# Where the sum of squares and the indexer's dots stand in TensorE's order, in a two-layer decoder trunk

## The chip, the cores and the metric

One NeuronCore of a Trainium2 chip runs the whole program in one launch. The metric is the device time of that launch in microseconds. TensorE multiplies matrices, VectorE and ScalarE move and transform results, GpSimd works on SBUF only, and SyncE issues the loads of the weights. The engines run side by side and wait for each other through semaphores.

## The reference

Two layers over 512 tokens of width 1024. Each layer has two gated feed-forward halves (width 2816) with a mixing stage between them.

```python
x = x + 0.5 * swiglu(rms_norm(x, ffn1_norm[l]), ffn1_gate[l], ffn1_up[l], ffn1_down[l])
h = rms_norm(x, mix_norm[l])
z = h @ w_in[l]         # queries, keys, values, indexer queries (4 heads), key, weights, pool, memory queries
# indexer, per block of 128 queries: dots = iq . ik ; score = sum_h w_h * relu(dots_h) ; top 128 keys
x = x + concat(y_attn, y_pool, y_mem) @ w_out[l]
x = x + 0.5 * swiglu(rms_norm(x, ffn2_norm[l]), ffn2_gate[l], ffn2_up[l], ffn2_down[l])
```

`rms_norm` divides by the root of the mean square over the 1024 channels. The kernel multiplies first and divides afterwards, when a product leaves PSUM, so the projections can start before the sum of squares is known.

## The kernel before, in words

Everything is float32. A matrix product takes three passes, high by high, high by low and low by high, where the high part is rounded to the multiplier's format by ScalarE and the low part is the rest (`passes`, L448; every matmul is recorded at L446). The activations are kept with channels on the partitions: 8 chunks of 128 channels by 512 tokens.

Weights come in slots of 128 x 1024 through a ring of four. SyncE loads a slot (L348), ScalarE rounds it (`round_ahead`, L883 to L891) when the slot's old user on TensorE is done (`slot_done`), GpSimd makes the low half (L382) and raises `w_ready`. One slot holds the weights of 24 matmuls. In ScalarE's program the roundings stand between the other work, so a rounding also waits for its turn.

A phase is a feed-forward half or a mixing stage; there are six. Each begins with `prepare`: ScalarE makes the high half of the activations and squares them (L871), VectorE makes the low half (L1097) and adds the squares of the 8 chunks in three additions (L1103 twice, L1105). TensorE starts with `project_first` (L462), which takes the first two slots and needs only the halves, and then `token_sums` (L508), one matmul with a matrix of ones into bank 4 that sums over the partitions. `root` (L877) takes the square root on ScalarE, `invert` (L1108) the reciprocal `r` on VectorE. Each evacuation multiplies by `r`.

In a feed-forward half the first gate and up products fill banks 0 and 1, the second (`gate_up(0, 1)`) banks 2 and 3. The first gate product in the loop may start when banks 0 and 1 are evacuated (`gu_free`, raised at L1138).

In the mixing stage the order on TensorE is: indexer queries (two slots, banks 0 and 1), the token sums, indexer key (bank 2), head weights (bank 3), value slots 0 and 1 (`project_v`, 8 blocks of three matmuls a slot, into banks 4 to 7), the transposition of `r` and of the head weights into columns (L612 to L618), the dots, value slots 2 and 3, the memory's sum, and then the query and key projections (`project_z`), into banks 0 to 3 in turn. Behind the third query slot, TensorE issues `heads_sum(0)` (L575), which needs the squares of the first query tile (ScalarE, L975), and that tile must first be evacuated by VectorE (L1156).

The dots are 12 products (three query blocks 1 to 3, four heads) of 256, 384 or 512 columns with a contraction over 64 rows. Heads 0 and 2 are on partitions 0 to 63, heads 1 and 3 on 64 to 127. They use banks 0 and 1 alternately, and product n waits for the ReLU of n - 2 (L952). ScalarE writes the ReLU to one of two buffers, VectorE adds it times its head weight to the score (L1193). VectorE then takes the largest scores, 8 at a time in 16 rounds (`take_largest`, L1199): six rounds ahead of the first query evacuation, then one round behind each.

All of it is in program order per engine; nothing is scheduled at run time.

Of the kernel before, what the change touches and what calls it, by code (L numbers as in the profile page):

```python
# [106 lines left out]
def build(nc, x_t, mem_t, weights, pool_w, params, consts, spreads, out):  # L107
# [93 lines left out]
    def sem(name):  # L201
        return nc.alloc_semaphore(name)
# [41 lines left out]
    mv_ready = sem("mv_ready")  # L244
    idx_hi_ready = sem("idx_hi_ready")
    idx_lo_ready = sem("idx_lo_ready")
    dots_done = sem("dots_done")
    relu_ready = sem("relu_ready")
    acc_score = sem("acc_score")
    bias_ready = sem("bias_ready")  # L250
# [89 lines left out]
    with nc.Block() as block:  # L340
# [103 lines left out]
        def _(pe):  # L444
# [10 lines left out]
            def weight(pos, at, n=P):  # L455
                s = slice(pos * SLOT + at, pos * SLOT + at + n)
                return w_hi[:, s], w_lo[:, s]
# [4 lines left out]
            def project_first(l, ph, n):  # L462


                def with_hi(i, k, part):
                    mm(bank[i][:, :], weight((n + i) % RING, k * P)[part], chunk(h_hi, k),
                       part == 0 and k == 0, False)

                def rounded(k):
                    pe.wait_ge(hi_ready, (l * 3 + ph) * DC + (k + 1))  # L470

                if ph == 0:

                    pe.wait_ge(w_hi_done, l * SLOTS + (n + 1))
                    for k in range(DC):
                        rounded(k)
                        with_hi(0, k, 0)
                        if k == 0:
                            pe.wait_ge(w_ready, l * SLOTS + (n + 1))
                        with_hi(0, k, 1)  # L480
                    pe.wait_ge(w_ready, l * SLOTS + (n + 2))
                    for k in range(DC):
                        for part in range(2):
                            with_hi(1, k, part)
                else:
                    pe.wait_ge(w_ready, l * SLOTS + (n + 2))
                    for k in range(DC):
                        rounded(max(k, 1))
                        for i in range(2):
                            for part in range(2):  # L490
                                with_hi(i, k, part)
                for i in range(2):
                    for k in range(DC):
                        if i == 0:
                            pe.wait_ge(lo_ready, (l * 3 + ph) * DC + (k + 1))
                        last = mm(bank[i][:, :], weight((n + i) % RING, k * P)[0], chunk(h_lo, k),
                                  False, k == DC - 1)
                    last.then_inc(slot_done, 1)
# [9 lines left out]
            def token_sums(l, ph):  # L508

                pe.wait_ge(consts_loaded, 16)  # L510
                pe.wait_ge(ssq_ready, l * 3 + (ph + 1))
                mm(bank[4][:, :], con(C_ONES, P), chunk(sq, 0)).then_inc(sum_done, 1)
# [11 lines left out]
            def ffn(l, e):  # L524
                ph, ffn_at = 2 * e, FFN_BASE[e]

                def gate_up(f, half):
                    n = ffn_at + 2 * half

                    pe.wait_ge(gu_free, (l * 2 + e) * FC + (f + (half + 1)))  # L530
                    at = l * SLOTS + ffn_at + f * 2 + 2 * half
                    for up in range(2):
                        pos = (n + up) % RING
                        pe.wait_ge(w_ready, at + (up + 1))
                        for k in range(DC):
                            last = passes(bank[2 * half + up][:, :], weight(pos, k * P),
                                          pair(h_hi, h_lo, k * T), k == 0, k == DC - 1)
                        last.then_inc(slot_done, 1)


                pe.wait_ge(gu_free, (l * 2 + e) * FC + 1)
                project_first(l, ph, ffn_at)
                token_sums(l, ph)
                gate_up(0, 1)
                with pe.Fori(1, FC // 2) as i:
                    gate_up(i * 2, 0)
                    gate_up(i * 2, 1)


                down_at = ffn_at + 2 * FC  # L550
                def down(f, off, start=False, stop=False, **part):
                    at = l * SLOTS + down_at + f + off
                    pe.wait_ge(w_ready, at + 1)

                    pe.wait_ge(a_lo_ready, (l * 2 + e) * FC + (f + (off + 1)))
                    fo = f * T + off * T
                    pos = (down_at + off + (f if isinstance(f, int) else 0)) % RING
                    accumulate(pos, a_hi[:, ds(fo, T)], a_lo[:, ds(fo, T)], start, stop, **part)

                pe.wait_ge(rms_ready, l * 3 + (ph + 1))  # L560
                down(0, 0, start=True, banks=range(4, DC))
                pe.wait_ge(gu_free, (l * 2 + e) * FC + (FC + 2))
                down(0, 0, start=True, banks=range(4), at=4)
                down(0, 1)
                with pe.Fori(0, (FC - 2) // RING - 1) as i:
                    for off in range(RING):
                        down(i * RING, 2 + off)
                for off in range(RING):
                    down(FC - RING, off, stop=off == RING - 1)

            def mix(l):
                def at(name, i=0):
                    return MIX_BASE[name] + i
# [14 lines left out]


                project_first(l, 1, at("iq"))  # L590
                token_sums(l, 1)
                project(l, at("ik"), bank[2][:, :], h_hi, h_lo)
                project(l, at("iw"), bank[3][:, :], h_hi, h_lo)

                pe.wait_ge(rms_ready, l * 3 + 2)

                def project_v(s):
                    n = at("av", s)
                    pe.wait_ge(w_ready, l * SLOTS + (n + 1))
                    for half in range(2):  # L600
                        k = 2 * s + half
                        whi, wlo = weight(n % RING, half * T, T)
                        for i in range(TT):
                            hhi, hlo = pair(h_hi, h_lo, k * T + i * P, P)
                            last = passes(bank[4 + i][:, :], (hhi, hlo), (whi, wlo),
                                          k == 0, k == DC - 1)
                    last.then_inc(slot_done, 1)

                project_v(0)
                project_v(1)  # L610
# [6 lines left out]
                              con(C_ID, 4, 4))  # L617
                last.then_inc(cols_done, 1)  # L618

                n = 0  # L620
                pe.wait_ge(idx_lo_ready, (l + 1) * 3)
                for i in range(1, TT):
                    for h in range(IDX_HEADS):
                        if n >= 2:
                            pe.wait_ge(relu_ready, l * 12 + (n - 1))
                        p0 = HD * (h % 2)
                        at_q = (h // 2) * T + i * P
                        q = [t[p0:p0 + HD, at_q:at_q + P] for t in (idx_hi, idx_lo)]
                        k = [t[p0:p0 + HD, 2 * T:2 * T + (i + 1) * P] for t in (idx_hi, idx_lo)]
                        passes(bank[n % 2][:, 0:(i + 1) * P], q, k, True, True)\  # L630
                            .then_inc(dots_done, 1)
                        n += 1
                project_v(2)
                project_v(3)

                pe.wait_ge(mssq_ready, l + 1)
                mm(bank[2][:, 0:MEM], con(C_ONES, P), sq[:, 0:MEM]).then_inc(msum_done, 1)


                def project_z(t, name, i):  # L640

                    if t < 6:
                        pe.wait_ge(relu_ready, (l + 1) * 12)
                    elif t == 6:
                        pe.wait_ge(mrms_ready, l + 1)
                    elif t == 7:
                        pe.wait_ge(cols_ready, l + 1)
                    else:
                        pe.wait_ge(proj_ready, l * 17 + (t - 3))
                    project(l, at(name, i), bank[t % 4][:, :], h_hi, h_lo)  # L650

# [206 lines left out]
        def _(act):  # L858
# [61 lines left out]
            def mix(l):  # L920
# [25 lines left out]
                n = 0  # L946
                for i in range(1, TT):
                    for h in range(IDX_HEADS):
                        act.wait_ge(dots_done, l * 12 + (n + 1))
                        if n >= 2:  # L950
                            act.wait_ge(acc_score, l * 12 + (n - 1))
                        nc.scalar.activation(chunk(t2, n % 2, T, (i + 1) * P), bank[n % 2][:, 0:(i + 1) * P],  # L952
                                             ACT.Relu, scale=HD ** -0.5 * IDX_HEADS ** -0.5)\
                            .then_inc(relu_ready, 1)
                        n += 1
# [501 lines left out]
```

## Time and profile before

| what | us |
| --- | --- |
| median of 3 runs | 2082.27 |
| lowest and highest of them | 2079.69 and 2084.04 |
| span of the profiled execution, first to last instruction | 2078.0 |
| TensorE busy in it | 2041.0 |
| VectorE, ScalarE, GpSimd busy | 755.7, 793.8, 891.0 |

The profile gives one execution. Of that execution only the span is listed, no separate time; the runs' median lies 4.3 above the span. Times in rows are microseconds from the start of the span. A matmul's end is modelled, so consecutive matmuls overlap in the rows.

### The profile page before, as it was taken

What the parts mean: (1) busy time and instruction counts of PE and PEld (TensorE: products, weight loads), DVE (VectorE), ACT (ScalarE), POOL (GpSimd) and SP (SyncE); (2) the same over time, 40 slices, a digit from 0 to 9 for tenths busy, and PEclk for the clock granted to TensorE, in tenths of its full rate; (3) what the DMA queues carried; (4) which work ended last, traced back from release to release, by engine and by line L of the source; (5) the groups of instructions that cost most, each with busy time, mean ns of one, the idle gap of its engine ahead of it and who ended that gap; (6) DMA issues with size and microseconds to landing.
All of it is one profiled execution on the core that took longest, in us unless ns stands there. A gap on an engine that the chain in (4) does not pass through costs nothing.

```text
span 2078.0 us, 27450 instructions
## 1 busy us (share of the span) xinstructions
PE 2041.0 (98%) x9256; PEld 1632.0 (79%) x9256; DVE 755.7 (36%) x1180; ACT 793.8 (38%) x1064; POOL 891.0 (43%) x404
## 2 busy tenths in 40 slices
PE   6999999999999999999989999999999999999999
PEld 5888888776767788888878888887767677888887
DVE  5333300675441633330063333006854425333201
ACT  5434321532452544432154443215325535444311
POOL 4444444433612444444354444444337034444442
PEclk9999999989899999999999999999899999999999
DMA  4222222312011222222222222223120022222222
GB/s 173 101 91 97 95 102 95 115 69 74 21 42 52 91 100 92 101 91 101 91 82 101 91 101 91 101 94 115 62 81 21 32 71 91 93 99 91 101 101 101
DMA packets 50567, 182.55 MB, mean 88 GB/s; under 512 B 5752, under 2 KB 6008, under 8 KB 50240
## 3 DMA queue, kind: packets, MB, share of 16 engines
q1 hardware_dynamic: 49824, 178.84, 24.7%
q10 hardware_dynamic: 672, 2.80, 0.4%
q8 instruction: 40, 0.66, 0.1%
q14 instruction: 31, 0.25, 0.0%
HBM read 179.52 MB, written 2.10 MB: 87 GB/s over the span
## 4 chain that ended last, share of the span: by engine, by line
PE 95%; DVE 3%; ACT 1%; issue 0%; DMA 0%; DVEq 0%; SPq 0%; ACTq 0%
PE bank L446 93%; PE bank L784 2%; DVE sq L1103 2%; DVE h_lo L1097 1%; DVE sq L1105 1%; ACT h_hi L863 0%; DMA x<-x_t 0%; ACT sq L871 0%; DVE x L1120 0%; DVEq L1097 0%; ACT t L952 0%; ACT L863 0%; DVEq L1096 0%; SPq L353 0%; ACTq L863 0%
## 5 line engine op out<-in xcount | busy, mean ns | idle before, releaser
L382 POOL TENSOR_TENSOR w_lo<-raw,w_hi 128x1024 fp32r<-128x1024 f32 x328 | 824.4, 2515 | 1141.8 <-ACT w_hi L891 1141.2
L891 ACT ACTIVATE w_hi<-raw 128x1024 fp32r<-128x1024 f32 x329 | 348.4, 1060 | 868.5 <-PE bank L446 868.0
L446 PE MATMUL bank<-h_hi,w_hi 128*128 128x512 f32 x1664 | 657.6, 395 | 12.0 <-ACT h_hi L863 12.0
L446 PE MATMUL bank<-h_hi,w_lo 128*128 128x512 f32 x1664 | 650.1, 391 | 0.0
L446 PE MATMUL bank<-h_lo,w_hi 128*128 128x512 f32 x1664 | 634.5, 390 | 0.0
L446 PEld LDWEIGHTS bank<-h_hi,w_hi 128*128 128x128 f32 x1664 | 314.3, 189 | 94.0 <-issue 16.2
L446 PEld LDWEIGHTS bank<-h_lo,w_hi 128*128 128x128 f32 x1664 | 313.9, 189 | 66.8 <-issue 2.4
L446 PEld LDWEIGHTS bank<-h_hi,w_lo 128*128 128x128 f32 x1664 | 314.1, 189 | 65.8
L446 PE MATMUL bank<-a_hi,w_hi 128*128 (+2 forms) x864 | 334.3, 387 | 0.0
L446 PE MATMUL bank<-a_hi,w_lo 128*128 (+2 forms) x864 | 332.8, 385 | 0.0
L446 PE MATMUL bank<-a_lo,w_hi 128*128 (+2 forms) x864 | 332.8, 385 | 0.0
L1120 DVE SCALAR_TENSOR_TENSOR x<-bank,x 128x512 f32<-128x512 f32 x48 | 32.7, 692 | 503.8 <-PE bank L446 503.8
L1138 DVE TENSOR_TENSOR t<-bank,r 128x512 f32<-128x512 f32 x88 | 60.8, 691 | 384.0 <-PE bank L446 384.0
L1144 DVE TENSOR_TENSOR a_lo<-t,a_hi 128x512 f32 x88 | 167.6, 1905 | 81.0 <-ACT a_hi L908 81.0
L446 PEld LDWEIGHTS bank<-a_hi,w_hi 128*128 128x128 f32 x864 | 162.3, 188 | 34.0 <-issue 2.1
L446 PEld LDWEIGHTS bank<-a_hi,w_lo 128*128 128x128 f32 x864 | 162.3, 188 | 32.6
L446 PEld LDWEIGHTS bank<-a_lo,w_hi 128*128 128x128 f32 x864 | 162.4, 188 | 32.0
L891 ACT ACT_TABLE_LOAD x45 | 57.7, 1283 | 138.7 <-PE bank L446 131.2
L1135 DVE TENSOR_TENSOR t<-bank,r 128x512 f32<-128x512 f32 x88 | 60.8, 691 | 91.5 <-PE bank L446 89.8
L908 ACT ACTIVATE a_hi<-t 128x512 f32 x88 | 55.6, 632 | 48.5 <-DVE t L1142 48.5
L1142 DVE TENSOR_TENSOR t<-t,t 128x512 f32<-128x512 f32 x88 | 61.3, 697 | 10.8
L905 ACT ACTIVATE t<-t 128x512 f32<-128x512 f32 x88 | 54.9, 624 | 12.6 <-DVE t L1135 12.1
(137 smaller groups left out, 1446.3 us busy)
## 6 DMA issues: line engine op xcount, KB each, us to landing
raw<-weights SPq DMA_DIRECT2D x332, 512.0 KB, 3.2
x<-x_t SPq DMA_DIRECT2D x4, 512.0 KB, 6.9
mem<-mem_t ACTq DMA_DIRECT2D x2, 1024.0 KB, 4.9
out_t<-x SPq DMA_DIRECT2D x8, 256.0 KB, 2.6
const<-consts SPq DMA_DIRECT2D x1, 505.5 KB, 9.8
spread_in<-spreads ACTq DMA_DIRECT2D x2, 216.0 KB
wpool<-pool_w ACTq DMA_DIRECT2D x2, 128.0 KB, 4.7
par<-params SPq DMA_DIRECT2D x1, 38.0 KB, 1.9
```

Of the source, the lines that this page charges most:

```text
L382: G.tensor_tensor(out=w_lo[:, s], in0=raw[:, s], in1=w_hi[:, s].bitcast(f32), op=ALU.subtract).then_inc(w_ready, 1)
L446: return nc.tensor.matmul(out_, lhsT, rhs, start=start, stop=stop, skip_group_check=True)
L784: last = nc.tensor.transpose(bank[2 + n % 2][:, b * P:(b + 1) * P], prob[n % 4][:, b * P:(b + 1) * P], con(C_ID, P))
L891: nc.scalar.activation(w_hi[:, s], raw[:, s], ACT.Copy).then_inc(w_hi_done, 1)
L905: nc.scalar.activation(g, g, ACT.Silu).then_inc(silu_ready, 1)
L908: nc.scalar.activation(a_hi[:, ds(f * T + half * T, T)], chunk(t2, half), ACT.Copy).then_inc(a_hi_ready, 1)
L1103: link(l, V.tensor_tensor(out=sq[:, 0:half], in0=sq[:, 0:half], in1=sq[:, half:2 * half], op=ALU.add))
L1120: V.scalar_tensor_tensor(out=chunk(x, j), in0=bank[j][:, :], scalar=scale, in1=chunk(x, j), op0=ALU.mult, op1=ALU.add)\
L1135: V.tensor_tensor(out=g, in0=bank[2 * half][:, :], in1=r[:, :], op=ALU.mult).then_inc(gate_ready, 1)
L1138: V.tensor_tensor(out=h, in0=bank[2 * half + 1][:, :], in1=r[:, :], op=ALU.mult).then_inc(gu_free, 1)
L1142: V.tensor_tensor(out=h, in0=g, in1=h, op=ALU.mult).then_inc(prod_ready, 1)
L1144: V.tensor_tensor(out=a_lo[:, ds(f * T + half * T, T)], in0=h, in1=a_hi[:, ds(f * T + half * T, T)].bitcast(f32), op=ALU.subtract).then_in ...
```

## The change

In a feed-forward half, `token_sums` is issued inside `gate_up(0, 1)`, after its gate matmuls and ahead of its up matmuls. In the mixing stage it is issued behind the projection of the indexer key.

The dots are split by query block. `dots(1)` stands ahead of value slot 2, `dots(2)` ahead of the block (1, 1) of slot 2, and `dots(3)` ahead of the block (0, 2) of slot 3. Each group writes banks 0 to 3, one for each head, and issues pass by pass, with the two heads of a pair alternating. Groups 2 and 3 wait once, for the four ReLUs of the group before. The wait for the columns' copy and the wait for all twelve ReLUs move ahead. There are two semaphores for finished dots, for even and for odd heads. Which operations run, and on what sizes, stays the same.

```diff
-                def gate_up(f, half):
+                def gate_up(f, half, between=None):
...
                         last.then_inc(slot_done, 1)
+                        if between is not None and up == 0:
+                            between()
...
                 project_first(l, ph, ffn_at)
-                token_sums(l, ph)
-                gate_up(0, 1)
+                gate_up(0, 1, lambda: token_sums(l, ph))
...
                 project_first(l, 1, at("iq"))
+                project(l, at("ik"), bank[2][:, :], h_hi, h_lo)
                 token_sums(l, 1)
-                project(l, at("ik"), bank[2][:, :], h_hi, h_lo)
                 project(l, at("iw"), bank[3][:, :], h_hi, h_lo)
...
+                        for i in range(TT):
+                            if before is not None and (half, i) in before:
+                                dots(before[half, i])
+                            last = v_block(n, s, half, i)
...
+                def dots(i):
+
+                    if i >= 2:
+                        pe.wait_ge(relu_ready, l * 12 + (i - 1) * IDX_HEADS)
+                    for hp in range(0, IDX_HEADS, 2):
+                        at_q = (hp // 2) * T + i * P
+                        for part, (tq, tk) in enumerate(((idx_hi, idx_hi), (idx_hi, idx_lo),
+                                                         (idx_lo, idx_hi))):
+                            for half in range(2):
+                                p = slice(half * HD, (half + 1) * HD)
+                                last = mm(bank[hp + half][:, 0:(i + 1) * P], tq[p, at_q:at_q + P],
+                                          tk[p, 2 * T:2 * T + (i + 1) * P], part == 0, part == 2)
+                                if part == 2:
+                                    last.then_inc(dots_done[half], 1)
...
-                n = 0
                 pe.wait_ge(idx_lo_ready, (l + 1) * 3)
-                for i in range(1, TT):
-                    for h in range(IDX_HEADS):
-                        if n >= 2:
-                            pe.wait_ge(relu_ready, l * 12 + (n - 1))
...
-                        passes(bank[n % 2][:, 0:(i + 1) * P], q, k, True, True)\
-                            .then_inc(dots_done, 1)
-                        n += 1
-                project_v(2)
-                project_v(3)
+                pe.wait_ge(cols_ready, l + 1)
+                project_v(2, {(0, 0): 1, (1, 1): 2})
+                project_v(3, {(0, 2): 3})
 
                 pe.wait_ge(mssq_ready, l + 1)
+                pe.wait_ge(relu_ready, (l + 1) * 12)
...
-                        act.wait_ge(dots_done, l * 12 + (n + 1))
+                        act.wait_ge(dots_done[h % 2], l * 6 + (n // 2 + 1))
...
-                        nc.scalar.activation(chunk(t2, n % 2, T, (i + 1) * P), bank[n % 2][:, 0:(i + 1) * P],
+                        nc.scalar.activation(chunk(t2, n % 2, T, (i + 1) * P), bank[h][:, 0:(i + 1) * P],
```

## Rows read from the trace of the kernel before

**Rows 1.** The page's busy line: us, share of the span, instructions.
```profile
PE 2041.0 (98%) x9256; PEld 1632.0 (79%) x9256; DVE 755.7 (36%) x1180; ACT 793.8 (38%) x1064; POOL 891.0 (43%) x404
```
**Rows 2.** Waits of TensorE: line waited for, us in total, times, longest.
```profile
PE bank L446 <- DVE sq L1105: 19.5, 6, 5.5
```
**Rows 3.** Timeline, TensorE, phase starts: start, us, instruction, [idle before, releaser].
```profile
29.12 1.97 PE L446 MATMUL bank<-sq,const 128*128 128x512 f32 x2 [3.99 <-DVE sq L1105]
...
394.46 2.08 PE L446 MATMUL bank<-sq,const 128*128 128x512 f32 x2 [3.50 <-DVE sq L1105]
...
690.29 3.79 PE L446 MATMUL bank<-h_lo,w_hi 128*128 128x512 f32 x16
695.55 1.12 PE L446 MATMUL bank<-sq,const 128*128 128x512 f32 x2 [1.47 <-DVE sq L1105]
...
1061.79 2.08 PE L446 MATMUL bank<-sq,const 128*128 128x512 f32 x2 [5.53 <-DVE sq L1105]
...
1427.91 1.30 PE L446 MATMUL bank<-sq,const 128*128 128x512 f32 x2 [3.50 <-DVE sq L1105]
```
**Rows 4.** Timeline, VectorE: evacuation of the second up product in three gate/up phases.
```profile
42.84 0.69 DVE L1138 TENSOR_TENSOR t<-bank,r 128x512 f32<-128x512 f32 x1 [1.24 <-PE bank L446]
...
707.62 0.69 DVE L1138 TENSOR_TENSOR t<-bank,r 128x512 f32<-128x512 f32 x1 [0.46 <-PE bank L446]
...
1076.29 0.69 DVE L1138 TENSOR_TENSOR t<-bank,r 128x512 f32<-128x512 f32 x1 [1.92 <-PE bank L446]
```
**Rows 5.** Timeline, ScalarE, VectorE, GpSimd behind the sum of the phase at 695.
```profile
696.71 0.69 ACT L880 ACTIVATE r<-bank,const 128x512 f32<-128x512 f32 x1 [6.07 <-PE bank L446]
...
697.43 3.35 DVE L1110 RECIPROCAL r<-r 128x512 f32<-128x512 f32 x1 [1.94 <-ACT r L880]
...
701.82 0.68 DVE L1138 TENSOR_TENSOR t<-bank,r 128x512 f32<-128x512 f32 x1
...
699.85 2.40 POOL L382 TENSOR_TENSOR w_lo<-raw,w_hi 128x1024 fp32r<-128x1024 f32 x1 [6.16 <-ACT w_hi L891]
```
**Rows 6.** Timeline, GpSimd: low half of ring slot 2, first phases of both layers.
```profile
21.69 3.55 POOL L382 TENSOR_TENSOR w_lo<-raw,w_hi 128x1024 fp32r<-128x1024 f32 x1 [4.60 <-ACT w_hi L891]
...
1052.84 5.07 POOL L382 TENSOR_TENSOR w_lo<-raw,w_hi 128x1024 fp32r<-128x1024 f32 x1 [4.60 <-ACT w_hi L891]
```
**Rows 7.** Timeline, mixing stage of layer one up to the column matmuls.
```profile
397.16 3.29 ACT L933 ACTIVATE a_hi<-mem,par 128x256 fp32r<-128x256 f32 x8
...
403.80 1.90 ACT L937 ACTIVATE sq<-mem 128x2048 f32<-128x2048 f32 x1
...
415.72 0.67 DVE L1156 TENSOR_TENSOR iw<-bank,r 4x512 f32<-4x512 f32 x1
...
418.96 1.05 PE L446 MATMUL bank<-const,r 1*128 1x1 f32 x8
```
**Rows 8.** Timeline, TensorE: first dots, first dot of block 3, return to the values.
```profile
420.83 0.39 PE L446 MATMUL bank<-idx_hi 64*128 64x256 f32 x2
...
427.22 0.79 PE L446 MATMUL bank<-idx_hi 64*128 64x512 f32 x1
...
431.79 0.80 PE L446 MATMUL bank<-w_hi,h_hi 128*128 128x512 f32 x1
```
**Rows 9.** Timeline: last score, first round, query evacuation, its square, its head sum.
```profile
432.83 0.75 DVE L1193 SCALAR_TENSOR_TENSOR score<-t,cols,score 128x512 f32<-128x512 f32 x1 [0.22 <-DVE score L1193]
434.09 1.48 DVE L1206 MAX8 top<-score 128x8 f32<-128x512 f32 x3 [0.51 <-DVE score L1193]
...
453.54 0.62 DVE L1156 TENSOR_TENSOR z<-bank,r 128x512 f32<-128x512 f32 x1
...
454.19 0.63 ACT L975 ACTIVATE t<-z 128x512 f32<-128x512 f32 x1 [2.51 <-DVE z L1156]
...
461.38 1.04 PE L446 MATMUL bank<-t,const 128*20 128x512 f32 x2
```
**Rows 10.** Busy us by engine in one stretch, then granted clock, DMA share, GB/s.
```profile
421.70:435.40 13.70, 13.26 (x39) 9.59 (x40) 9.18 (x15) 6.93 (x13) 0.86 (x1) 0.50 0.11 39
```

More of the change, by code:

```diff
@@ L246, in build @@
     idx_lo_ready = sem("idx_lo_ready")
-    dots_done = sem("dots_done")
+    dots_done = [sem("dots_even_done"), sem("dots_odd_done")]
     relu_ready = sem("relu_ready")
@@ L590, in mix, with v_block, project_v @@
                 project_first(l, 1, at("iq"))
+                project(l, at("ik"), bank[2][:, :], h_hi, h_lo)
                 token_sums(l, 1)
-                project(l, at("ik"), bank[2][:, :], h_hi, h_lo)
                 project(l, at("iw"), bank[3][:, :], h_hi, h_lo)
                 pe.wait_ge(rms_ready, l * 3 + 2)
-                def project_v(s):
+                def v_block(n, s, half, i):
+                    k = 2 * s + half
+                    hhi, hlo = pair(h_hi, h_lo, k * T + i * P, P)
+                    return passes(bank[4 + i][:, :], (hhi, hlo), weight(n % RING, half * T, T),
+                                  k == 0, k == DC - 1)
+                def project_v(s, before=None):
                     n = at("av", s)
@@ L600, in project_v @@
                     for half in range(2):
-                        k = 2 * s + half
-                        whi, wlo = weight(n % RING, half * T, T)
                         for i in range(TT):
-                            hhi, hlo = pair(h_hi, h_lo, k * T + i * P, P)
-                            last = passes(bank[4 + i][:, :], (hhi, hlo), (whi, wlo),
-                                          k == 0, k == DC - 1)
+                            if before is not None and (half, i) in before:
+                                dots(before[half, i])
+                            last = v_block(n, s, half, i)
                     last.then_inc(slot_done, 1)
+                def dots(i):
[11 more added lines that the diff above has]
+                                    last.then_inc(dots_done[half], 1)
                 project_v(0)
@@ L618, in mix @@
                 last.then_inc(cols_done, 1)
-                n = 0
                 pe.wait_ge(idx_lo_ready, (l + 1) * 3)
-                for i in range(1, TT):
-                    for h in range(IDX_HEADS):
-                        if n >= 2:
-                            pe.wait_ge(relu_ready, l * 12 + (n - 1))
[L626 to L629, printed above, removed]
-                        passes(bank[n % 2][:, 0:(i + 1) * P], q, k, True, True)\
-                            .then_inc(dots_done, 1)
-                        n += 1
-                project_v(2)
-                project_v(3)
+                pe.wait_ge(cols_ready, l + 1)
+                project_v(2, {(0, 0): 1, (1, 1): 2})
+                project_v(3, {(0, 2): 3})
                 pe.wait_ge(mssq_ready, l + 1)
+                pe.wait_ge(relu_ready, (l + 1) * 12)
                 mm(bank[2][:, 0:MEM], con(C_ONES, P), sq[:, 0:MEM]).then_inc(msum_done, 1)
                 def project_z(t, name, i):
-                    if t < 6:
-                        pe.wait_ge(relu_ready, (l + 1) * 12)
-                    elif t == 6:
+                    if t == 6:
                         pe.wait_ge(mrms_ready, l + 1)
-                    elif t == 7:
-                        pe.wait_ge(cols_ready, l + 1)
-                    else:
+                    elif t >= 8:
                         pe.wait_ge(proj_ready, l * 17 + (t - 3))
```

## The prediction

> **What bounds the kernel now.** I read the page's busy line first: TensorE is busy 98% of a span of 2078.0 us, no other engine over 43% [rows 1]. So the time is TensorE's instruction count times its pace, plus what stops it. The list of who waited for whom leaves one stop that matters: TensorE waits for the last addition of the sum of squares, six times, 19.5 us in all [rows 2]. The timeline of TensorE at five of the six phase starts shows each: 3.99, 3.50, 1.47, 5.53 and 3.50 us idle before the matmul with the ones (the sixth repeats the third) [rows 3]. A matmul's row is 0.39 us long but the next starts after (3.79-0.39)/15 = 0.227 us [rows 3], so an "idle" of the profile understates the lost time by 0.16. I call T0 the moment at which the array could take the next matmul: sum row, minus idle, minus 0.16, which gives 24.97, 390.80, 693.92 and 1056.10.
>
> 24 matmuls (one weight slot) take 5.44 us at that pace. In the second gate/up phase the evacuation of the second pair starts at 707.62 [rows 4]: 13.70 after T0 = 1.63 wait + 10.88 for two slots + 1.19. Of the 1.19 I give 1.0 to the sum itself and 0.2 to the release of the reader. The same subtraction for the first phase gives 17.87 = 4.15 + 10.88 + 1.19 + 1.65 left, and for layer two 20.19 = 5.69 + 10.88 + 1.19 + 2.43 left [rows 3, 4]. What is left is half clock after the wait.
>
> The second place is the indexer's dots: 36 small matmuls hold TensorE from 420.83 to 431.79 [rows 8], and the granted clock there and in the value projection behind it is 0.50 for 13.7 us [rows 10], its lower level of 1.2 GHz. Between dots TensorE waits for ScalarE to empty one of two banks.
>
> **Edit one, gate/up phases.** The gate's 24 matmuls go ahead of the wait. Before, both halves (10.88 us) covered the chain from the sum to the freed bank; now only the up half does. That chain, from [rows 3, 5]: sum at 695.55, square root on ScalarE at 696.71, reciprocal on VectorE 697.43 to 700.78, gate and up evacuated by 701.82 + 0.68 = 702.50: 6.95 us, with its release 7.0. Cover is 1.0 + 5.44 = 6.44, so a new wait of about 0.55 us arises at the first looped gate. Its weights are no later: the low half on GpSimd ends at 699.85 + 2.40, 6.70 after the sum. So the next gate starts at (end of moved gate) + 7.0, against (evacuation row - 0.2) before.
> - First phase: slot 2 of the ring is ready at 21.69 + 3.55 = 25.24 [rows 6], 0.3 after T0. 25.28 + 5.44 + 7.0 = 37.72 against 42.64: 4.9 saved.
> - Second gate/up phase of a layer: slot ready. 693.92 + 5.44 + 7.0 = 706.36 against 707.42: 1.1 saved, twice.
> - Layer two's first: the slot is ready only at 1052.84 + 5.07 = 1057.91 [rows 6], so 1.8 of the wait stays as a wait for weights. 1057.95 + 12.44 = 1070.39 against 1076.09: 5.7 saved.
>
> Sum: 12.7 us. No DMA changes order; weight loads are released by rounding, which follows TensorE, and land in a few us against 5.44 per slot.
>
> **Edit two, key projection ahead of the sum.** T0 = 390.80. Keys to 396.24 (the sum's input was ready at 394.4, no wait left), sum to 397.2, head weights to 402.7, two value slots to 413.5. Before, they ended just ahead of 418.96 [rows 7]: 5.4 earlier. But the column matmuls wait for the evacuation of the head weights, which ended at 415.72 + 0.67 = 416.39, at the end of VectorE's queue: additions over the memory's squares, eight low halves, three index low halves. Its start hangs on ScalarE's square of the memory at 403.80 [rows 7], which waited for the key slot; now it follows square root (397.4), eight high halves (3.29) and one rounding (1.06), so about 402.2, 1.6 earlier. The evacuation ends at about 414.8: a new wait of 1.3 us. Columns 1.9 us [rows 7, 8], then about 0.3 for the copy that dots now wait for: the dots start at D = 417.1 against 420.83.
>
> **Edit three, dots.** Two heads sit in different halves of the rows. The first two products start together: two in 0.39 us [rows 8]. So 12 matmuls of 256, 384, 512 columns cost 6 pairs: 0.68, 1.02, 1.36 us at full clock, 3.06 together; one after the other they would be 6.12. Into and out of small products I add 0.35 a group (after the last one the next large matmul starts some 0.1 late, and the second product of a head some 0.1 late, by the spacing around [rows 8]). I take 4.1, near the pairs, since the row is of the same operation. Value slots 2 and 3 are 16 blocks of 0.68 = 10.88. They end at E = D + 15.0 = 432.1, against 431.79 + 10.88 + about 1.8 of half clock = 444.5: 12.4 earlier.
> Dots group 2 needs group 1's four activations. All twelve took 12.75 us before (420.83 to 432.83 + 0.75) [rows 8, 9], about 1.06 a head, 4.2 for four; it comes at D + 4.4. No wait.
>
> The Trainium skill ("TensorEngine Tiling (Array Packing)", Key Properties) says that changing the tiling mode drains TensorE, which speaks against splitting one stretch of small matmuls into three. The trace shows such a change as about 0.1 us. By the rule alone there are four more changes a layer, and at that price the sum loses under 1 us, which the 0.35 holds.
>
> **What is late next.** The selection on VectorE starts when the last score is added. Before, that was 433.58, 10.9 us ahead of the end of the value projection; now group 3 starts at D + 1.0 + 3.4 + 1.4 + 3.4 = D + 9.2. From its first matmul to the last addition were 6.4 us (427.22 to 433.58) at half clock, about 5.3 at full. Scores end at D + 14.5, only 0.5 ahead of E. Then 0.5, six rounds and a reciprocal up to the first query evacuation, 434.09 to 453.54 = 19.45, and its square ready 454.19 + 0.63 = 454.82, 1.3 behind [rows 9]: D + 35.75 = 452.85. TensorE reaches the first head sum, behind three query slots, at E + 0.3 + 16.4 = D + 31.7. New wait: about 4 us, where there were 6.5 us of slack. Head sum: 461.38 [rows 9] to 452.85, 8.5 saved. VectorE needs 3.6 a tile against 5.44 of TensorE, so it catches up and nothing waits again. Two layers: 17.0.
>
> Clock. A wait of 4.15 us cost 1.65 behind it, 5.69 cost 2.43, 1.63 cost nothing [rows 3, 4]. The new 4 us cost 1.65 a layer: 3.3. The 1.3 wait, the one-row column matmuls and the 0.3 are low activity like the stretch after which the clock fell at 421.7 [rows 10]; dots between full-size blocks should lift it. Bounds 0 and 2.4 a layer; I take 0.8: 1.6.
> The Trainium skill ("TensorE: Matmul & The Clock Gate", HAM oscillation) has it that idle gaps close the gate and the work behind them runs at half rate; the trace agrees for gaps of 3.66 us and up. By it the new wait costs what is charged above; without it the sum would be 3.3 better.
>
> **Sum.** 12.7 + 17.0 - 3.3 - 1.6 = 24.8 us off a span of 2078.0: 2053.2. Of the profiled execution only the span is given; the median of the runs, 2082.27, lies 4.3 above it. Forecast: 2057.5.
>
> **Rivals.**
> - A, the selection does not hold TensorE (it hides as it did). For it: VectorE had 6.5 us of slack. Against: that slack was made by the scores ending 10.9 us early. The gain is then that at E: 2 x 12.4 + 12.7 - 1.6 = 35.9: 2046.5.
> - B, the clock stays at half level through both value slots, since small matmuls now come three times. For it: four stretches of low activity in a row, [rows 10]. Against: 5 full blocks between groups, and the clock rose 3.6 us after blocks resumed at 431.79. 15.0 us of work become 28, E = D + 28, head sum at D + 45; 7.5 a layer worse than forecast, of which 1.6 is charged: 24.8 - 15 + 1.6 = 11.5: 2071. The Trainium skill (same page, psum-queue depth-cycling) has a kernel whose short idles between bank groups made the clock oscillate; that would be B.
> - C, slower: the same half clock reaches from the columns through the query slots to the first head sum. 31.7 us at 1.88 times is D + 59.6, against 461.38 = D + 44.3: 15.3 lost a layer; 30.6 - 12.7 = 18 slower: 2100. It decides from some 22 us of full-clock work per layer run at half. Before, the clock recovered each time within four us of dense work.
> - D, the change does not do what it says: the moved gate only moves the wait (the chain longer than 7.0, or weights late), leaving the mix gain alone or half of all: 12 us, 2070.
>
> **Chances.** Forecast 0.64 (its own range 2051 to 2064), A 0.12, B 0.12, C 0.05, D 0.07. Range 2046 to 2070: low end A, high end just short of B and D; their halves outside and C are about 0.15. A measurement tells no change within 0.2%, 4.2 us. Slower takes C: 0.05; within 0.2%, the tails of B and D: 0.04; faster 0.91.
>
> **What would show it.** Right: no wait for the sum of squares but 1.8 at layer two's weights; waits of 0.5 for the up evacuation, 1.3 for the head-weight evacuation, about 4 for the first query square; dots 4 us a layer; clock 1.00 in the value slots. Wrong: no wait at the first head sum (A), clock 0.5 over the value slots (B), a wait over 1.5 behind the up half (D).

## The result and the profile after

The changed kernel takes 2065.68 us (median of 4 runs, 2063.15 to 2067.45) against 2080.98 for the kernel before (4 runs). The ratio is 0.9924, 95% interval 0.9909 to 0.9938: 15.3 us faster. The profiled execution took 2067.45 with a span of 2065.6, so what lies around a span is 1.85 us. Its span is 12.4 under that of before.

The list of who waited for whom, for TensorE, the whole span (line waited for, us in total, times, longest); of before it showed [rows 2]:

```profile
PE bank L446 <- ACT h_hi L871: 12.0, 1, 12.0
PE bank L446 <- ACT t L983: 7.8, 2, 3.9
PE bank L446 <- DVE iw L1164: 6.5, 2, 3.2
PE bank L446 <- DVE t L1146: 2.1, 4, 0.6
PE bank L446 <- DVE h_lo L1105: 1.7, 1, 1.7
PE bank L446 <- DVE cols L1190: 0.9, 2, 0.5
```

The 19.5 us for the sum of squares are gone. Five kinds of wait have come: 3.9 a layer for the square of the first query tile, 3.2 a layer for the evacuated head weights, 0.5 four times for the up evacuation, 1.7 once for the low half of the activations, 0.45 a layer for the columns' copy. (The first line is the start of the program, 12.0 before too.)

TensorE in the timeline, first phase and the mixing stage of layer one (start, us, instruction, idle before); they answer to [rows 3, 7, 8, 9]:

```profile
21.98 3.79 PE L446 MATMUL bank<-h_lo,w_hi 128*128 128x512 f32 x16
...
31.05 1.02 PE L446 MATMUL bank<-sq,const 128*128 128x512 f32 x2
...
38.10 0.49 PE L446 MATMUL bank<-h_hi,w_hi 128*128 128x512 f32 x1 [0.55 <-DVE t L1146]
...
382.78 3.79 PE L446 MATMUL bank<-h_lo,w_hi 128*128 128x512 f32 x16
...
391.85 1.02 PE L446 MATMUL bank<-sq,const 128*128 128x512 f32 x2
...
412.47 1.05 PE L446 MATMUL bank<-const,r 1*128 1x1 f32 x8 [3.24 <-DVE iw L1164]
...
415.62 0.58 PE L446 MATMUL bank<-idx_hi 64*128 64x256 f32 x2 [0.45 <-DVE cols L1190]
...
427.18 0.50 PE L446 MATMUL bank<-idx_hi 64*128 64x512 f32 x2
...
428.44 0.40 PE L446 MATMUL bank<-idx_hi,idx_lo 64*128 64x512 f32 x2
428.76 0.50 PE L446 MATMUL bank<-w_hi,h_hi 128*128 128x512 f32 x1
```

With T0 as in the prediction (here 25.61, 386.41, 689.16, then 1052.5, 1413.23, 1711.69), the span's stages compare so:

| stage | before | after | saved | forecast |
| --- | --- | --- | --- | --- |
| start to first T0 | 24.97 | 25.61 | -0.6 | 0 |
| first gate/up half | 365.83 | 360.80 | 5.0 | 4.9 |
| mixing, layer one | 303.12 | 302.75 | 0.4 | 6.0 |
| second half and layer two's first | 730.33 | 724.07 | 6.3 | 6.8 |
| mixing, layer two | 298.86 | 298.46 | 0.4 | 6.0 |
| last half | 354.89 | 353.94 | 0.9 | 1.1 |

The gate/up phases gave 12.2 of the 12.7 forecast. The two mixing stages gave 0.8 of 12.1.

Inside layer one's mixing stage, counted from T0: the columns start at 26.06 (28.16 before, 24.04 forecast), the dots at 29.21 (30.03 before, 26.3 forecast), the first head sum at 67.43 (70.58 before, 62.05 forecast), and the next phase's T0 is at 302.75 (303.12). So of the forecast head start of 5.4 us, 3.3 are lost ahead of the columns and 1.3 more ahead of the dots, and of 3.15 saved at the head sum 2.8 are lost behind it.

**Ahead of the columns.** VectorE's and GpSimd's timeline, the first two of the eight low halves of the memory, each by itself, then the next two, and then GpSimd:

```profile
402.42 2.62 DVE L1178 SCALAR_TENSOR_TENSOR a_lo<-mem,par,a_hi 128x256 fp32r<-128x256 f32 x1
404.96 2.68 DVE L1178 SCALAR_TENSOR_TENSOR a_lo<-mem,par,a_hi 128x256 fp32r<-128x256 f32 x1
407.57 0.87 DVE L1178 SCALAR_TENSOR_TENSOR a_lo<-mem,par,a_hi 128x256 fp32r<-128x256 f32 x2
...
402.13 2.63 POOL L382 TENSOR_TENSOR w_lo<-raw,w_hi 128x1024 fp32r<-128x1024 f32 x1 [1.89 <-ACT w_hi L899]
404.97 2.39 POOL L382 TENSOR_TENSOR w_lo<-raw,w_hi 128x1024 fp32r<-128x1024 f32 x1 [0.22 <-ACT w_hi L899]
```

Each takes under 0.5 us where nothing is beside it (two in 0.87), and 2.6 where a GpSimd instruction runs: both end within 0.3 us of GpSimd's. The eight together took 7.60 us, against 5.42 before, when one GpSimd instruction fell on them. These 2.2 us are why the head weights came 1.9 to 2.1 us later than forecast. The Trainium skill ("GPSIMD Engine Reference", its table of specifications) names it: GpSimd shares its SBUF interfaces with VectorE, with contention for VectorE instructions that have two SBUF inputs. The trace agrees, and gives the price.

**From the columns to the scores, and behind the head sum.** Busy us by engine, then granted clock, DMA share, GB/s, four stretches of the changed kernel's layer one:

```profile
413.30:420.10 6.80, 6.35 (x29) 5.46 (x30) 2.12 (x5) 1.43 (x4) 0.72 (x1) 0.51 0.23 77
453.80:457.30 3.50, 3.46 (x7) 1.91 (x8) 3.50 (x11) 1.52 (x3) 2.38 (x1) 0.59 0.00 0
...
540.00:560.00 20.00, 20.00 (x118) 14.46 (x117) 7.08 (x21) 9.81 (x26) 17.49 (x24) 0.84 0.00 1
...
620.00:640.00 20.00, 20.00 (x92) 13.62 (x92) 4.54 (x16) 4.89 (x14) 0.00 (x0) 0.70 0.00 0
```

and two stretches of before that answer to the last two:

```profile
547.50:567.50 20.00, 20.00 (x86) 13.89 (x85) 5.85 (x17) 6.43 (x16) 16.66 (x23) 0.64 0.01 1
...
627.50:645.00 17.50, 17.50 (x106) 12.21 (x106) 5.57 (x22) 6.38 (x21) 0.00 (x0) 1.00 0.01 1
```

The clock was at its lower level from the column matmuls through the first dots into the value blocks, for 6.8 us where before it was for 13.7 [rows 10]; it fell again behind the wait at the head sum; and in the attention units, which the change doesn't touch, it was lower in one place and higher in another than before. The two stretches of before start 7.5 us later, as the head sum does.

**The selection.** The last score and the first query's evacuation (VectorE), its square (ScalarE) and its head sum (TensorE), as in [rows 9]:

```profile
431.80 0.75 DVE L1201 SCALAR_TENSOR_TENSOR score<-t,cols,score 128x512 f32<-128x512 f32 x1 [0.22 <-DVE score L1201]
433.06 1.48 DVE L1214 MAX8 top<-score 128x8 f32<-128x512 f32 x3 [0.51 <-DVE score L1201]
...
452.49 0.63 DVE L1164 TENSOR_TENSOR z<-bank,r 128x512 f32<-128x512 f32 x1
...
453.16 0.63 ACT L983 ACTIVATE t<-z 128x512 f32<-128x512 f32 x1 [13.01 <-DVE z L1164]
```

From last score to square ready are 21.24 us, exactly as before. The scores end 16.9 us after the first dots (12.75 before, 14.5 forecast).

### The profile page after: what moved, and what is told of

It reads as the page before. It is cut to its first block, busy times and chain, and to the rows that moved or that the text cites. A ratio compares the mean times of both kernels' runs of the same rounds, so it can differ in the third digit from the quotient of the medians.

```text
span 2065.6 us, 27440 instructions
## 1 busy us (share of the span) xinstructions
PE 2030.5 (98%) x9256; PEld 1625.5 (79%) x9256; DVE 762.3 (37%) x1180; ACT 791.8 (38%) x1064; POOL 889.0 (43%) x404
## 4 chain that ended last, share of the span: by engine, by line
PE 93%; DVE 3%; issue 2%; ACT 1%; DVEq 0%; DMA 0%; SPq 0%; ACTq 0%
PE bank L446 91%; PE bank L792 2%; DVE r L1118 1%; DVE a_lo L1178 0%; DMA x<-x_t 0%; DVE score L1201 0%; ACT a_hi L941 0%; DVE h_lo L1105 0%; DVE score L1217 0%; DVE top L1214 0%; DVE sq L1171 0%; ACT sq L945 0%; DVE idx_lo L1185 0%; ACT r L888 0%; ACT h_hi L871 0%
## 5 line engine op out<-in xcount | busy, mean ns | idle before, releaser
L446 PEld LDWEIGHTS bank<-h_hi,w_hi 128*128 128x128 f32 x1664 | 314.1, 189 | 96.9 <-issue 15.3
L913 ACT ACTIVATE t<-t 128x512 f32<-128x512 f32 x88 | 54.9, 624 | 12.6 <-DVE t L1143 12.1
```

What stands on the lines that cost most here:

```text
L446: return nc.tensor.matmul(out_, lhsT, rhs, start=start, stop=stop, skip_group_check=True)
L913: nc.scalar.activation(g, g, ACT.Silu).then_inc(silu_ready, 1)
```

## The experiments

Each ran in five rounds against the kernel before; the times of before in the three groups are 2082.34, 2079.94 and 2082.91. The differences from the changed kernel below are between medians of different groups, so 1 or 2 us in them mean nothing. "Up to the first head sum" is counted from the mixing stage's T0 in the profiled execution (70.6 and 70.9 us in the two layers of before, 67.4 in both of the changed kernel), "behind it" from there to the next phase's T0.

### Which edit brings what

Sum moved in the gate/up phases alone (the diff's edit to `gate_up` on the kernel before):

> The kernel before with the sum moved in the four gate/up phases alone. Theory (the gate/up edit brings nearly all, the mixing edits nearly nothing): span 12 us under the kernel before, about 2066, the same as the changed kernel within 2; four new waits of 0.55 us for the up evacuation; both mixing stages 303 and 299 us from first free slot to the next phase's, as before. Rival (the mixing edits bring their forecast share and the gate/up edit less): 5 us or less under the kernel before.

Measured: 2071.48, ratio 0.9952 (0.9935 to 0.9968). The profiled execution, the quickest of six, had a span of 2065.6, 12.4 under the profiled one of before. There are four waits for the up evacuation, 2.1 us together, and the mixing stages' two waits of 3.5 for the sum of squares stay. The gate/up stages up to layer two's mixing give 11.3 us, as in the changed kernel, which is what the theory says of them. Two things differ from it: the median is 5.8 us over the changed kernel's, not within 2, and the mixing stages took 298.8 and 301.4 us, not 303 and 299, though nothing was changed in them.

Both moves of the sum, dots as before:

```diff
                 project_first(l, 1, at("iq"))
+                project(l, at("ik"), bank[2][:, :], h_hi, h_lo)
                 token_sums(l, 1)
-                project(l, at("ik"), bank[2][:, :], h_hi, h_lo)
```

> Both moves of the sum, with the dots as they were: one stretch, two banks. Theory (the split of the dots takes from the mixing stage what the earlier key projection gives it): the wait for the head weights is there (3 us), the columns start some 2 us earlier than before, no wait at the first head sum, so 2 us a layer over the first experiment: 16 us under the kernel before, 2062, faster than the changed kernel by 3 to 4. Rival (split dots are a gain by themselves and the losses are elsewhere): 2068 to 2072, slower than the changed kernel.

Measured: 2067.46, ratio 0.9936 (0.9917 to 0.9956). Within its interval this is the changed kernel's time without the split dots. The wait for the head weights is there, 3.2 a layer, and there is none at the first head sum. It is not the 3 to 4 us faster than the changed kernel that I expected; the intervals can't tell which of the two is ahead. In the profiled executions the changed kernel is 2.4 us ahead in each layer up to the first head sum (67.4 against 69.8), and behind it this one is 7.6 us quicker over both layers, with the same instructions.

Split dots alone:

```diff
-                gate_up(0, 1, lambda: token_sums(l, ph))
+                token_sums(l, ph)
+                gate_up(0, 1)
...
+                token_sums(l, 1)
                 project(l, at("ik"), bank[2][:, :], h_hi, h_lo)
-                token_sums(l, 1)
```

> The split dots alone, both sums where they were. Theory (TensorE saves the dots' waits but gives them back at the first head sum, behind the selection, and in half clock): wait of 2 to 4 us at the first head sum, 0 to 2 us a layer saved, span 2074 to 2078. Rival (the split saves its 8 us a layer and only the head weights' wait eats it in the changed kernel): 2062 to 2064.

Measured: 2079.87, ratio 0.9987 (0.9978 to 0.9997): 2.7 us. It has the same 3.9 us wait at the first head sum in both layers, with no late head weights in the way. Up to the first head sum it saves 2.4 and 3.0 us. So the split by itself saves about 1 us a layer, and the late head weights can't be the reason, since there are none here.

### The wait for the head weights

In the changed kernel, ScalarE's roundings of value slot 3 and query slot 0 are held, so GpSimd's low halves come later:

```diff
+                act.wait_ge(proj_ready, l * 17 + 4)
                 round_ahead(l, MIX_BASE["iw"])
                 round_ahead(l, MIX_BASE["av"])
```

> The changed kernel with two of ScalarE's roundings (value slot 3, query slot 0) held until the head weights are evacuated, so that GpSimd's two low halves no longer run beside VectorE's eight low halves of the memory. Theory (a VectorE instruction that meets a GpSimd one waits for its end, two such meetings of 2.2 us): the eight take 3.4 us in place of 7.6, the wait for the head weights goes from 3.2 to under 0.5, the columns run at full clock, 3.5 to 6 us a layer faster than the changed kernel: 2054 to 2059. Rival (the eight are long for another reason, their input or ScalarE beside them): still 7 us, the wait stays near 3, no gain.

Measured: 2058.41, ratio 0.9883 (0.9864 to 0.9903), 7.3 us under the changed kernel. VectorE and GpSimd in its timeline:

```profile
402.83 3.26 DVE L1179 SCALAR_TENSOR_TENSOR a_lo<-mem,par,a_hi 128x256 fp32r<-128x256 f32 x8
...
413.04 1.70 DVE L1202 SCALAR_TENSOR_TENSOR score<-t,cols,const 128x256 f32<-128x256 f32 x1 [1.30 <-ACT t L961]
414.95 2.30 DVE L1202 SCALAR_TENSOR_TENSOR score<-t,cols,score 128x256 f32<-128x256 f32 x1 [0.22 <-DVE score L1202]
...
409.78 7.19 POOL L382 TENSOR_TENSOR w_lo<-raw,w_hi 128x1024 fp32r<-128x1024 f32 x3 [9.13 <-ACT w_hi L899]
```

All eight low halves take 3.26 us with GpSimd away, and no wait for the head weights is left. The collisions have moved to two score additions, 1.70 and 2.30 in place of 0.48, where the next group of dots is not yet due (one wait of 1.2 us in two layers). The edit moves ScalarE's roundings too, but in the changed kernel ScalarE stood idle from 404.89 to 409.27, while the second long low half ran (404.96 to 407.64). This settles the meeting with GpSimd as the cause of the late head weights.

### The wait at the first head sum

Selection rounds spread, in the changed kernel:

```diff
-FIRST_ROUNDS = ROUNDS - ZT
+FIRST_ROUNDS = 2
+TILE_ROUNDS = [2] * 4 + [1] * 6
...
-                    take_largest(l * DVE_CHAIN + links[0])
-                    links[0] += ROUND_CHAIN
+                    for _ in range(TILE_ROUNDS[j]):
+                        take_largest(l * DVE_CHAIN + links[0])
+                        links[0] += ROUND_CHAIN
```

> The changed kernel with VectorE's selection rounds spread: two ahead of the first query evacuation in place of six, two behind each of the first four tiles. Theory (the wait at the first head sum is the selection's six rounds, now 12 us shorter to the first tile): the wait of 3.9 us goes in both layers, and the half clock behind it; 4 to 6 us a layer, 2054 to 2058. No new wait, since two rounds and an evacuation (6.6) stand against a projection and a head sum (6.4), with 7 us of slack at the start. Rival (TensorE is held by something behind it, and the wait moves to the next head sums or to a bank): under 3 us in all.

Measured: 2059.22, ratio 0.9887 (0.9866 to 0.9907): 6.5 under the changed kernel. The wait is gone in both layers and none has come in its place. The gain is below the 8 to 12 us expected. Up to the first head sum the profiled execution saves 2.8 and 4.0 us; it had three long stretches of half clock in the attention units.

Groups of dots nearer:

```diff
-                project_v(2, {(0, 0): 1, (1, 1): 2})
-                project_v(3, {(0, 2): 3})
+                project_v(2, {(0, 0): 1, (0, 3): 2})
+                project_v(3, {(0, 0): 3})
```

> The changed kernel with three blocks between the first two groups of dots and five before the third, in place of five and five. Theory (the scores end later because VectorE idles 4.3 us between groups 1 and 2 and 1.7 between 2 and 3): scores end about 1.5 to 2.5 us earlier after the first dots, the wait at the first head sum falls to 1.5 to 2.5 us, 1.4 to 2.5 us a layer, 2061 to 2064. Rival (TensorE then waits for the activations ahead of group 2): a new wait of 1 us or more there and no gain.

Measured: 2064.74, ratio 0.9917 (0.9899 to 0.9935), not to be told from the changed kernel. The wait fell from 7.8 to 5.1 us for both layers, 2.6 a layer where 1.5 to 2.5 was expected:

```profile
PE bank L446 <- ACT t L983: 5.1, 2, 2.6
```

The spacing sets when the scores end, but 1.3 us a layer is too little to show.

### Both remedies

The held roundings and the spread rounds together:

> The held roundings and the spread selection together. Theory (two separate waits, one behind the other on TensorE): the gains add, 7 from the held roundings and 8 to 12 from the selection, 2046 to 2051; no wait over 1.3 us in the mixing stages but the columns' copy. Rival (the first saving is taken back at the second place): not below 2055.

Measured: 2045.14 (2043.23 to 2047.89), ratio 0.9828 (0.9809 to 0.9847). This is the best version, 20.5 us under the changed kernel, more than the 7.3 and 6.5 of the two remedies alone. TensorE's waits in it:

```profile
PE bank L448 <- ACT h_hi L873: 12.1, 1, 12.1
PE bank L448 <- DVE t L1149: 2.1, 4, 0.5
PE bank L448 <- POOL w_lo L384: 1.9, 2, 1.7
PE bank L448 <- DVE cols L1193: 0.9, 2, 0.5
```

Its mean granted clock is 0.992, of the changed kernel 0.988: 17 us less at the lower level (2 x 0.008 x 2043 = 33 against 2 x 0.012 x 2066 = 50), worth about half of that, 8 us, by estimate. The surplus of 6.7 us is of that size. Up to the first head sum the two gains nearly add: 9.5 and 6.8 us over both layers apart, 17.2 together. The rest of the surplus arises behind it, where the two layers took 461.8 us, against 466.2 to 467.4 in the changed kernel and with either remedy alone. That this comes of the remedies and not by chance is not shown.

Not all of the half clock ahead of the value slots goes with the late head weights. The best version in layer one, behind its first dots (busy us by engine, clock, DMA share, GB/s):

```profile
411.80:415.10 3.30, 3.30 (x18) 2.59 (x15) 2.26 (x2) 1.04 (x3) 3.30 (x2) 0.52 0.49 159
```

That is 3.3 us at the lower level in place of 6.8; the columns ran at 1.00. (In layer two of the run with the held roundings alone the clock stayed at 1.00 there, so the fall is not certain either.)

With the groups nearer as well:

> The last one with the groups nearer as well. Theory (with the selection no longer holding TensorE, where the groups stand does not matter): the same as without, within 2 us. Rival (nearer groups make TensorE wait for the activations): 2 to 4 us slower.

Measured: 2054.67 (2049.94 to 2058.69), ratio 0.9875 (0.9853 to 0.9897): 9.5 slower than without, so the theory fell. TensorE now waits for the activations ahead of a group:

```profile
PE bank L448 <- ACT t L963: 3.8, 2, 2.5
```

That is 3.8 us; GpSimd's held instructions stand on the score additions that those activations follow. The mean clock is 0.988, which by the same estimate is 8 us, so the two more than cover the loss.

Old dots, both moves of the sum, held roundings, the selection as before:

> Both moves of the sum and the held roundings, with the dots in one stretch on two banks as before and the selection as before. Theory (once its two waits are taken away, the split of the dots is worth what was forecast for TensorE, some 5 to 8 us a layer): this stands at the second experiment's time less 5 to 7, about 2061, that is 12 to 17 us slower than the split dots with both remedies (2045). Rival (the split is worth little even then, and the held roundings and the rest do it): within 6 us of 2045.

Measured: 2066.74, ratio 0.9927 (0.9907 to 0.9947): 21.6 slower than the best version, where I expected 12 to 17. The held roundings gave next to nothing here, 0.7 us. Their collisions fall on score additions which the old dots wait for one by one:

```profile
PE bank L446 <- ACT t L954: 6.7, 6, 1.5
```

Up to the first head sum the best version is 10.0 us a layer ahead of this one (58.8 against 68.8), and that is nearly all of the difference. There was no wait at the head sum here for spread rounds to take away. So with its two waits removed the split of the dots is worth about 10 us a layer. Against the kernel before, the best version reaches the head sum 11.8 and 12.1 us earlier: that is close to rival A, which had 12.4 less 0.8 for the clock.

Heads of a pair one after the other in the best version:

```diff
-                        for part, (tq, tk) in enumerate(...):
-                            for half in range(2):
+                        for half in range(2):
+                            for part, (tq, tk) in enumerate(...):
```

> The version with both remedies, but within a group each head's three products are issued in a row, as before, in place of the two heads of a pair alternating. Theory (heads of a pair overlap only when their instructions alternate, since now no wait separates the pairs): a group of 512 columns takes 2.2 to 2.7 us in place of 1.6, 2 to 3 us a layer on TensorE, 2049 to 2051. Rival (the two halves of the rows overlap in either order, as the kernel before showed for its first two heads): no difference, 2045 within 2.

Measured: 2047.49, ratio 0.9828 (0.9813 to 0.9843), the same. The two row halves overlap in either order; in the kernel before only the wait between the two heads had kept them apart. Its third group of dots:

```profile
423.16 0.50 PE L448 MATMUL bank<-idx_hi 64*128 64x512 f32 x2
423.49 0.40 PE L448 MATMUL bank<-idx_lo,idx_hi 64*128 64x512 f32 x2
423.73 0.40 PE L448 MATMUL bank<-idx_hi,idx_lo 64*128 64x512 f32 x2
```

## Why the prediction was right or wrong

The direction was right and 2065.68 lies in the range of 2046 to 2070, but outside the 2051 to 2064 of the forecast itself, nearer to rival D's 2070, whose mechanism did not happen. The forecast of 2057.5 gave 24.8 us where 15.3 came. From span to span, which is what the sum was made of, only 12.4 came, half of it. The two profiled executions lie differently in their runs (2079.85 and 2067.45 beside medians of 2080.98 and 2065.68), and adding 4.3 us to a span, where 1.85 lies around it, made the forecast 2.4 too long. So the number missed by 8.2 and the sum by 12.4. By its steps:

1. **The wait for the sum of squares goes, a chain of 7.0 us takes its place: right.** Sum at 31.05, next gate at 38.10: 7.05. New wait 0.55, four times. 12.2 us for 12.7.
2. **Layer two's slot of weights keeps 1.8 of the wait: right in size, but in the profiled execution by luck.** There the low half of the activations met GpSimd and cost a wait of 1.70, the weights none. The first experiment shows the forecast form, 1.7 for `w_lo`.
3. **"The evacuation ends at about 414.8: a new wait of 1.3 us": this term was mis-sized.** The wait was 3.2 (3.4 from slot to slot). The sum took the eight low halves at their 5.42 us of before. Of that duration 2.2 were a collision (3.26 without any), and moving TensorE ahead moved GpSimd's next instruction onto them too. The held roundings show it. 2.1 us a layer.
4. **The dots cost 4.1 us of TensorE: right.** Group 3 took 428.76 - 427.18 = 1.58 for 1.7, group 2 the same way 1.3 for 1.4.
5. **"Bounds 0 and 2.4 a layer; I take 0.8" for half clock: mis-sized.** Columns and first dots ran at half clock for 6.8 us, columns to dots took 3.15 us for the 2.2 taken, and the scores came 2.4 us later behind the first dots than forecast. That is 3.3 us in layer one and 3.2 in layer two, above the upper bound. The late head weights are about half of it: without them 3.3 us at the lower level are left in the best version, which cost 1.6, still twice the 0.8.
6. **A wait of about 4 us at the first head sum: right,** 3.9. Its two ends, TensorE's arrival and the square, both came 2.4 us later behind the first dots than forecast (34.15 for 31.7, 38.17 for 35.75), so the half clock did not show in it. Rival A is out. The spread rounds show that the selection causes it.
7. **1.65 behind it for the clock:** 2.8 and 3.2 us were lost from the head sum to the next phase. The fall is there (0.59 in the 3.5 us behind, 1.4 us); the rest lies in the attention units, whose clock differs from run to run. The stretch behind the head sum has the same matmuls in every kernel here, and it took 232.5 and 227.9 us in the two layers of before and 227.9 to 235.3 in all of them. The mean of six such stretches behind a wait of 3.9 us is 233.4, of sixteen without a wait 231.4: 2.0, near the 1.65, but within a spread of 7. How much of the rest the change causes is open.

Three terms, 3, 5 and 7, make up the 5.7 us by which layer one's mixing stage fell short: 2.0 for columns later than forecast, 3.3 less the 0.8 charged for the clock, and 2.8 less 1.65 behind the head sum. Rivals B and C did not happen: the clock was at 1.00 through most of the two value slots. Rival D did not either, by the chain of 7.05.

## What to carry to other kernels

When a wait is removed from the critical engine, redo the timeline of the helper engines from there: what moves earlier may meet something that it did not meet before. A duration of before that is longer than its like beside it (2.6 against 0.47) may be a collision, and then must not be carried over as the instruction's price. And a chain with 6.5 us of slack is the next bound once its start is tied to a later place: spread its work before splitting what feeds it.

## What the runs showed of the hardware

- A VectorE instruction with two SBUF inputs that starts beside a running 2.4 us GpSimd `tensor_tensor` ends with it: 0.47 becomes 2.6 us, for as little as 256 columns. Where VectorE was already at work it was the other way: the three index low halves from 409.94 took 1.88 us, against 1.90 with GpSimd away, and the GpSimd instruction that started among them at 410.40 took 3.62 in place of 2.4.
- Products over partitions 0 to 63 and 64 to 127 overlap fully, whether issued alternately or three and three: twelve of 512 columns in 1.6 us at full clock.
- In the attention units, with the same instructions, a stretch of half clock came or stayed away: the last of them, near the end of layer one's stage, had 0.70 in the changed kernel and 1.00 before. Mean clocks of 0.983 to 0.992 go with times 37 us apart, of which about half is clock (an estimate: 0.009 more of 2060 us, times two for the time at the lower level, is 37 us there, and half of that is lost).
